# The up projections of a float32r transformer kernel: one moving operand of 512 columns for the activation's hi and lo halves

## The chip, the cores and the metric

The kernel runs on one core of one Trainium2 chip. The metric is the device time of one execution in microseconds; the kernel before takes 1380.37 us, the median of 3 runs (1379.97 to 1382.86).

## The reference

Three transformer layers over 256 tokens of width 1024 (batch 1), float32. The first block mixes a causal convolution, a stick-breaking attention and a cross-attention to a memory, then comes its feed-forward part; two hybrid layers (forgetting attention and retention) follow, each with the same feed-forward part between two layer norms. What the change touches is in all three:

```python
D_FF = 4 * D_MODEL                                                   # 4096
h2 = rms_norm(x, g_mlp[l])                                           # first block
x = x + jnp.square(jax.nn.relu(h2 @ w_up[l])) @ w_down[l]
...
hid = jnp.square(jax.nn.relu(jnp.einsum('bsd,df->bsf', x, w_ff1)))   # hybrid layers
ff = jnp.einsum('bsf,fd->bsd', hid, w_ff2)
return layernorm(DEEPNORM_ALPHA * x + ff, ln2_g, ln2_b)
```

## The kernel before

Every large product is computed in float32r with both operands split into a rounded high part and a remainder: w = w_hi + w_lo, x = x_hi + x_lo. Three products are kept, w_hi x_hi + w_lo x_hi + w_hi x_lo, so each 128 x 128 weight tile costs three matmuls of 256 moving columns (the 256 tokens).

Weights come in halves of 128 x 2048 (1 MB): eight contraction tiles of 256 columns for most products, four of 512 for the down projections. SP loads a half into one of two raw slots when the remainder of the half two before it is made (`lo_ready`). ACT copies it to `w_hi` (L251), DVE subtracts to `w_lo` (L619). `w_hi` and `w_lo` are rings of four halves; ACT overwrites a slot when TensorE has finished the half four before (`gemm_done`). All engines take the halves in one order written out by hand, and each engine takes its instructions in order.

PSUM is held as `gps` and `aps`, four banks of 512 columns each. `rows_first` (L1201) computes one up half, that is 256 rows of the hidden layer: `rows_part` (L1176) sends the output rows 0 to 127 to the left half of one `gps` bank and 128 to 255 to the right half, 48 matmuls on line L1182. With `split_count` (the first half after a norm) it goes through pairs of contraction tiles, both row blocks at a time: it waits for the pair's hi part, issues 8 matmuls, waits for its lo part, issues 4.

The feed-forward part (`ffn` on each engine) has 16 units, one per up half: on TensorE the halves 0 and 1 (units 0, 1), 2 and 3 (units 2, 3), then two down halves, and so on in turn: up pair, down pair, with the down pair always one up pair behind. Units 0 and 1 go into `gps` banks 0 and 1, units 2 and 3 into banks 2 and 3, and so on in turn; a bank is free when ACT has applied the relu of the unit four before (`ffn_relu`), so the first four wait for no bank. The down halves (L1274, L1277, L1279) accumulate in the four banks of `aps` over the whole feed-forward part and wait for `hidden`.

A unit's evacuation: ACT relu from PSUM to `staged` (L317), ACT square to `Q_hi` (L321); DVE squares `staged` into `hid_s` (L772) and subtracts `Q_hi` to give `Q_lo` (L776). On ACT and DVE the order is: split of halves 2 and 3; unit 0; split of half 4; unit 1; split of half 5; then in a loop unit, split, unit, split, split, split. In the hybrid layers DVE splits half 1 after the layer norm (L1152); in the first block all of that is done before the norm ends. `R_hi` and `R_lo`, the inputs of the up projections, come pair by pair from the norm: ACT writes hi (L286, L309), DVE lo (L681, L763).

Of the kernel before, what the change touches and what calls it, by code (L numbers as in the profile page):

```python
# [20 lines left out]
P = 128  # L21
# [53 lines left out]
def build(nc, mem_t, x_t, w1, w2, wf, par1, par2, con1, con2, out_t):  # L75
    with ExitStack() as ctx:
# [3 lines left out]
        def sem(name):  # L80
# [8 lines left out]
        R_hi, R_lo = sb("R_hi", [P, KT, T], F32R), sb("R_lo", [P, KT, T], F32R)  # L89
# [70 lines left out]
            mg mg_hi mg_lo ffn_relu ffn_sq ffn_hi hidden  # L160
# [82 lines left out]
        def _(act):  # L243
# [18 lines left out]
            def two(ap):  # L262
                return ap.rearrange("p (a t) -> p a t", a=2)
# [48 lines left out]
            def up(h, l, uu, par_, a, fresh=False):  # L312

                act.wait_ge(s["gemm_done"], h + (l + 1))
                if not fresh:
                    act.wait_ge(s["ffn_sq"], uu - 1)
                act.activation(staged[:, a, :], gps[:, 2 * par_ + a, :], ACT.Relu)\  # L317
                   .then_inc(s["ffn_relu"], 1)
                act.wait_ge(s["ffn_relu"], uu + 1)
                t0 = 4 * par_ + 2 * a  # L320
                act.activation(Q_hi[:, t0:t0 + 2, :], two(staged[:, a, :]), ACT.Square)\  # L321
                   .then_inc(s["ffn_hi"], 1)
# [290 lines left out]
        def _(dve):  # L613
# [155 lines left out]
            def up(uu, par_, a):  # L769
                t0 = 4 * par_ + 2 * a  # L770
                dve.wait_ge(s["ffn_relu"], uu + 1)
                dve.tensor_tensor(hid_s[:, a, :], staged[:, a, :], staged[:, a, :], ALU.mult)\  # L772
                   .then_inc(s["ffn_sq"], 1)
                dve.wait_ge(s["ffn_sq"], uu + 1)
                dve.wait_ge(s["ffn_hi"], uu + 1)
                dve.tensor_tensor(Q_lo[:, t0:t0 + 2, :], two(hid_s[:, a, :]),  # L776
# [398 lines left out]
        def _(pe):  # L1175
# [72 lines left out]
            def ffn(h0, l0, ub, split_count, ln=None):  # L1248

                def up(h, l, par_, free_sem, free_count):  # L1250
                    for a in range(2):

                        pe.wait_ge(free_sem, free_count + a)
                        rows_first(h, l + a, 2 * par_ + a, R_hi, R_lo,
                                   split_count if free_sem is not s["ffn_relu"] else None)
# [28 lines left out]
                relu = s["ffn_relu"]  # L1284
                for a in range(2):
                    rows_first(h0, l0 + a, a, R_hi, R_lo, split_count if a == 0 else None)
                for a in range(2):
                    rows_first(h0, l0 + 2 + a, 2 + a, R_hi, R_lo)
                down(h0, l0 + 4, 0, ub + 2, first=True)
                with pe.Fori(0, 3) as f:  # L1290
                    hf, uf = h0 + f * 8, ub + f * 4
                    up(hf, l0 + 6, 0, relu, uf + 1)
                    down(hf, l0 + 8, 1, uf + 4)
                    up(hf, l0 + 10, 1, relu, uf + 3)
# [151 lines left out]
            with pe.Fori(0, LAYERS) as ly:  # L1446
# [82 lines left out]
                pe.wait_ge(s["ffn_relu"], ly * 16 + 16)  # L1529
# [181 lines left out]
```

## Time and profile before

| | |
|---|---|
| median of 3 runs | 1380.37 us (1379.97 to 1382.86) |
| profiled execution: span (its own time is given as this alone) | 1381.2 us |
| TensorE busy (matmuls) | 1309.6 us, 95% |
| TensorE busy (weight loads) | 1257.4 us, 91% |
| DVE busy | 808.1 us, 59% |
| ACT busy | 647.6 us, 47% |
| mean granted TensorE clock | 0.984 |
| mean DMA rate | 155 GB/s |

A row of the groups reads: line, engine, operation, output and inputs, shapes, count, then busy time in us, mean ns of one, and the idle time of the engine just before. A matmul's duration holds its way through the array too, so that neighbours overlap; the pace of a stream is read from the distance of the starts. The feed-forward parts lie at about 451 to 640 us, 804 to 993 us and 1170 to 1359 us.

### The profile page before, as it was taken

To read this page: it belongs to the slowest core of one execution; us is meant where nothing else is said; L and a number is where in the kernel's file an instruction comes from. 1 tells how busy PE (TensorE), PEld (TensorE's weight loads), DVE (VectorE), ACT (ScalarE), POOL (GpSimd) and SP (SyncE) were. 2 spreads that over 40 slices of the span, in tenths; PEclk is the share of its full clock that TensorE was granted. 3 is DMA by queue.
4 is the path that set the end of the run, shared out by engine and by line. 5 is a ranking of instruction groups with operands and counts; after the bars stand their busy time and mean duration, and the time that the engine had idled before them with its cause. 6 is when DMAs were issued, how large, how long until landed. Compare 5 with 4: busy or idle time off the path is not lost.

```text
span 1381.2 us, 24664 instructions
## 1 busy us (share of the span) xinstructions
PE 1309.6 (95%) x10264; PEld 1257.4 (91%) x10264; DVE 808.1 (59%) x905; ACT 647.6 (47%) x722; POOL 0.2 (0%) x4
## 2 busy tenths in 40 slices
PE   5999999999999999999999979999889997999994
PEld 5999999999998999999888879999888896999994
DVE  5666965745555745454565666454656657655555
ACT  4565555664443534343434445444254444544443
POOL 0000000000000000000000000000000000000000
PEclk9999999999999999999999999999999999999998
DMA  6653444444554454553523226555233321565550
GB/s 222 214 184 123 157 149 150 157 149 156 183 184 153 153 188 178 186 209 125 183 92 123 92 100 224 195 178 187 91 143 136 116 99 61 183 214 186 179 183 31
DMA packets 34354, 214.58 MB, mean 155 GB/s; under 512 B 4576, under 2 KB 8672, under 8 KB 8800
## 3 DMA queue, kind: packets, MB, share of 16 engines
q1 hardware_dynamic: 34272, 213.37, 43.7%
q8 instruction: 65, 1.06, 0.3%
q14 instruction: 17, 0.14, 0.0%
HBM read 212.31 MB, written 1.05 MB: 154 GB/s over the span
## 4 chain that ended last, share of the span: by engine, by line
PE 85%; DVE 6%; ACT 3%; issue 3%; DMA 2%; SPq 0%; DVEq 0%; ACTq 0%
PE gps L1182 50%; PE aps L1279 7%; PE aps L1277 7%; PE aps L1274 7%; PE gps L1220 2%; PE gps L1221 2%; PE gps L1222 2%; DMA raw<-w 2%; DVE w_lo L619 1%; PE aps L1315 1%; ACT w_hi L251 1%; PE aps L1462 1%; PE aps L1483 1%; PE gps L1228 1%; ACT B L304 1%
## 5 line engine op out<-in xcount | busy, mean ns | idle before, releaser
L619 DVE TENSOR_TENSOR w_lo<-raw,w_hi 128x2048 fp32r<-128x2048 f32 x204 | 454.1, 2229 | 285.9 <-ACT w_hi L251 285.5
L251 ACT ACTIVATE w_hi<-raw 128x2048 fp32r<-128x2048 f32 x204 | 378.5, 1857 | 231.9 <-PE aps L1279 123.9
L1182 PE MATMUL gps<-R_hi,w_hi 128*128 128x256 f32 x896 | 238.2, 287 | 18.7 <-ACT R_hi L309 11.8
L1182 PE MATMUL gps<-H_hi,w_hi 128*128 128x256 f32 x896 | 241.3, 291 | 12.6 <-ACT H_hi L309 5.9
L1182 PE MATMUL gps<-R_hi,w_lo 128*128 128x256 f32 x896 | 236.9, 286 | 0.0
L1182 PE MATMUL gps<-H_hi,w_lo 128*128 128x256 f32 x896 | 236.5, 285 | 0.0
L1274 PE MATMUL aps<-Q_hi,w_hi 128*128 128x256 f32 x768 | 217.7, 283 | 0.0
L1277 PE MATMUL aps<-Q_lo,w_hi 128*128 128x256 f32 x768 | 217.3, 283 | 0.0
L1279 PE MATMUL aps<-Q_hi,w_lo 128*128 128x256 f32 x768 | 217.3, 283 | 0.0
L1182 PEld LDWEIGHTS gps<-R_hi,w_hi 128*128 128x128 f32 x896 | 175.0, 195 | 20.5 <-ACT R_hi L309 12.6
L1182 PEld LDWEIGHTS gps<-H_hi,w_hi 128*128 128x128 f32 x896 | 174.2, 194 | 15.1 <-issue 7.4
L1182 PE MATMUL gps<-H_lo,w_hi 128*128 128x256 f32 x896 | 179.9, 285 | 0.0
L1182 PE MATMUL gps<-R_lo,w_hi 128*128 128x256 f32 x896 | 179.5, 285 | 0.0
L1182 PEld LDWEIGHTS gps<-H_hi,w_lo 128*128 128x128 f32 x896 | 174.3, 195 | 1.1 <-issue 1.0
L1182 PEld LDWEIGHTS gps<-R_hi,w_lo 128*128 128x128 f32 x896 | 174.9, 195 | 0.0
L1274 PEld LDWEIGHTS aps<-Q_hi,w_hi 128*128 128x128 f32 x768 | 147.4, 192 | 0.1
L1277 PEld LDWEIGHTS aps<-Q_lo,w_hi 128*128 128x128 f32 x768 | 147.4, 192 | 0.1
L1279 PEld LDWEIGHTS aps<-Q_hi,w_lo 128*128 128x128 f32 x768 | 147.4, 192 | 0.0
L1182 PEld LDWEIGHTS gps<-H_lo,w_hi 128*128 128x128 f32 x896 | 140.3, 194 | 0.0
L1182 PEld LDWEIGHTS gps<-R_lo,w_hi 128*128 128x128 f32 x896 | 140.3, 194 | 0.0
L1182 PE MATMUL gps<-Q_hi,w_hi 128*128 128x256 f32 x320 | 85.1, 292 | 3.1 <-ACT Q_hi L601 3.1
L317 ACT ACTIVATE staged<-gps 128x512 f32<-128x512 f32 x48 | 28.5, 594 | 115.0 <-PE gps L1182 115.0
(229 smaller groups left out, 1654.2 us busy)
## 6 DMA issues: line engine op xcount, KB each, us to landing
raw<-w SPq DMA_DIRECT2D x198, 1024.0 KB, 4.8
B<-x_t SPq DMA_DIRECT2D x2, 512.0 KB, 4.5
B<-mem_t SPq DMA_DIRECT2D x1, 1024.0 KB, 7.7
B<-x_t SPq DMA_DIRECT2D x1, 1024.0 KB, 7.8
B<-con SPq DMA_DIRECT2D x1, 1024.0 KB, 6.8
out_t<-B SPq DMA_DIRECT2D x1, 1024.0 KB, 4.4
cst<-con SPq DMA_DIRECT2D x1, 320.0 KB, 4.8
raw<-wf SPq DMA_DIRECT2D x6, 16.0 KB, 1.6
```

Source lines behind the costliest of these rows:

```text
L251: act.activation(w_hi[:, ring(l), 0:n], raw[:, raw_slot(l), 0:n], ACT.Copy)\
L304: ins = act.activation(X[:, k, :], B1[:, k, :], ACT.Identity, bias=lpar[:, b + k:b + k + 1], scale=lpar[:, g + k:g + k + 1])
L317: act.activation(staged[:, a, :], gps[:, 2 * par_ + a, :], ACT.Relu)\
L619: dve.tensor_tensor(w_lo[:, ring(l), 0:n], raw[:, raw_slot(l), 0:n], w_hi[:, ring(l), 0:n].bitcast(F32), ALU.subtract)\
L1182: return pe.matmul(gps[:, bank_, nt * T:(nt + 1) * T], w[:, r, c:c + P], op[:, k, :], start=start, stop=stop, skip_group_check=True)
L1220: pe.matmul(out, xh, wh, start=(k == 0), stop=False)
L1221: pe.matmul(out, xh, wl, start=False, stop=False)
L1222: ins = pe.matmul(out, xl, wh, start=False, stop=(k == KT - 1))
L1228: ins = pe.matmul(out, ones, src[:, k, 0:T], start=(start and k == tiles[0]), stop=(stop and k == tiles[-1]))
L1274: pe.matmul(out, w_hi[:, r, c:c + P], hh, start=(first and k == 0 and nt % 2 == 0), stop=False, skip_group_check=True)
L1277: pe.matmul(out, w_hi[:, r, c:c + P], hl, start=False, stop=False, skip_group_check=True)
L1279: ins = pe.matmul(out, w_lo[:, r, c:c + P], hh, start=False, stop=(last and k == 3 and nt % 2 == 1), skip_group_check=True)
```

## The change

The two halves of the up projections' input become one tile `R` with hi and lo as its first index, so that `R[:, :, k, :]` is a moving operand of 512 columns: 256 of hi and 256 of lo. For each contraction tile and row block `up` issues a matmul of 512 columns with the `w_hi` tile, and one of 256 columns with the `w_lo` tile and `R_hi` into the left half of the same bank. A unit's two row blocks now fill two banks (unit a of a pair: banks 2a and 2a + 1), and the sum of the left and right halves is the projection. ACT copies the right halves of both banks to `staged`; DVE adds the left halves from PSUM into `hid_s`, then computes max(h, 0) h into `staged`; ACT copies that to `Q_hi`; DVE subtracts to `Q_lo`. TensorE waits, from the third unit of a feed-forward part on, for the DVE sum of the unit two before (`ffn_sum`). The first half of a feed-forward part waits, for each pair of contraction tiles, for hi and lo at once, in its first row block only, and goes through row block 0 entirely before row block 1.

```diff
--- before.py
+++ after.py
@@ -86,7 +86,8 @@
         w_lo = sb("w_lo", [P, 4, HALF], F32R)
 
         H_hi, H_lo = sb("H_hi", [P, KT, T], F32R), sb("H_lo", [P, KT, T], F32R)
-        R_hi, R_lo = sb("R_hi", [P, KT, T], F32R), sb("R_lo", [P, KT, T], F32R)
+        R = sb("R", [P, 2, KT, T], F32R)
+        R_hi, R_lo = R[:, 0, :, :], R[:, 1, :, :]
         Q_hi, Q_lo = sb("Q_hi", [P, KT, T], F32R), sb("Q_lo", [P, KT, T], F32R)
         B1, B2, B3 = (sb(f"B{i}", [P, KT, T]) for i in (1, 2, 3))
         B4 = sb("B4", [P, KT, T + 2])
@@ -157,7 +158,7 @@
             sb_z sb_sp sb_soft sb_lb sb_t sb_arg sb_e sb_a sb_o sb_ohi sb_olo
             hsq hn_sum hn_var hn_log hn_row hn_norm
             cx_s cx_max cx_exp cx_p cx_t cx_pt cx_o cx_oe ox_hi ox_lo
-            mg mg_hi mg_lo ffn_relu ffn_sq ffn_hi hidden
+            mg mg_hi mg_lo ffn_corr ffn_sum ffn_sq ffn_hi hidden
             f_cols f_gate f_logit f_sp f_m fx_s fx_l fx_max fx_e fx_p fx_t fx_pt fx_o fx_ohi fx_oe
             rt_mm rt_x rn_s rn_m rn_o rn_oe gn_mean gn_c gn_sq gn_var gn_v gn_log gn_y gn_hi gn_lo""".split()
         s = {n: sem(n) for n in names}
@@ -313,12 +314,12 @@
 
                 act.wait_ge(s["gemm_done"], h + (l + 1))
                 if not fresh:
-                    act.wait_ge(s["ffn_sq"], uu - 1)
-                act.activation(staged[:, a, :], gps[:, 2 * par_ + a, :], ACT.Relu)\
-                   .then_inc(s["ffn_relu"], 1)
-                act.wait_ge(s["ffn_relu"], uu + 1)
+                    act.wait_ge(s["hidden"], uu - 1)
+                act.activation(two(staged[:, a, :]), gps[:, 2 * a:2 * a + 2, T:2 * T], ACT.Copy)\
+                   .then_inc(s["ffn_corr"], 1)
+                act.wait_ge(s["ffn_sq"], uu + 1)
                 t0 = 4 * par_ + 2 * a
-                act.activation(Q_hi[:, t0:t0 + 2, :], two(staged[:, a, :]), ACT.Square)\
+                act.activation(Q_hi[:, t0:t0 + 2, :], two(staged[:, a, :]), ACT.Copy)\
                    .then_inc(s["ffn_hi"], 1)
 
             def ffn(h0, l0, ub, first=False):
@@ -768,12 +769,15 @@
 
             def up(uu, par_, a):
                 t0 = 4 * par_ + 2 * a
-                dve.wait_ge(s["ffn_relu"], uu + 1)
-                dve.tensor_tensor(hid_s[:, a, :], staged[:, a, :], staged[:, a, :], ALU.mult)\
-                   .then_inc(s["ffn_sq"], 1)
+                dve.wait_ge(s["ffn_corr"], uu + 1)
+                dve.tensor_tensor(two(hid_s[:, a, :]), gps[:, 2 * a:2 * a + 2, 0:T], two(staged[:, a, :]),
+                                  ALU.add).then_inc(s["ffn_sum"], 1)
+                dve.wait_ge(s["ffn_sum"], uu + 1)
+                dve.scalar_tensor_tensor(staged[:, a, :], hid_s[:, a, :], 0.0, hid_s[:, a, :],
+                                         ALU.max, ALU.mult).then_inc(s["ffn_sq"], 1)
                 dve.wait_ge(s["ffn_sq"], uu + 1)
                 dve.wait_ge(s["ffn_hi"], uu + 1)
-                dve.tensor_tensor(Q_lo[:, t0:t0 + 2, :], two(hid_s[:, a, :]),
+                dve.tensor_tensor(Q_lo[:, t0:t0 + 2, :], two(staged[:, a, :]),
                                   Q_hi[:, t0:t0 + 2, :].bitcast(F32), ALU.subtract)\
                    .then_inc(s["hidden"], 1)
 
@@ -1247,12 +1251,24 @@
 
             def ffn(h0, l0, ub, split_count, ln=None):
 
-                def up(h, l, par_, free_sem, free_count):
+                def up(h, l, summed, gate_at=None):
                     for a in range(2):
-
-                        pe.wait_ge(free_sem, free_count + a)
-                        rows_first(h, l + a, 2 * par_ + a, R_hi, R_lo,
-                                   split_count if free_sem is not s["ffn_relu"] else None)
+                        if summed is not None:
+                            pe.wait_ge(s["ffn_sum"], summed + a)
+                        pe.wait_ge(s["lo_ready"], h + (l + a + 1))
+                        r = ring(l + a)
+                        for nt in range(2):
+                            out = gps[:, 2 * a + nt, :]
+                            for k in range(KT):
+                                if gate_at is not None and a == nt == 0 and k % 2 == 0:
+                                    pe.wait_ge(gate_at[0], gate_at[2] + (k // 2 + 1))
+                                    pe.wait_ge(gate_at[1], gate_at[2] + (k // 2 + 1))
+                                c = k * 256 + nt * P
+                                pe.matmul(out, w_hi[:, r, c:c + P], R[:, :, k, :], start=(k == 0),
+                                          stop=False, skip_group_check=True)
+                                ins = pe.matmul(out[:, 0:T], w_lo[:, r, c:c + P], R_hi[:, k, :], start=False,
+                                                stop=(k == KT - 1), skip_group_check=True)
+                        ins.then_inc(s["gemm_done"], 1)
 
                 def down(h, l, par_, uu, first=False, last=False):
 
@@ -1281,17 +1297,14 @@
                                                 skip_group_check=True)
                         ins.then_inc(s["gemm_done"], 1)
 
-                relu = s["ffn_relu"]
-                for a in range(2):
-                    rows_first(h0, l0 + a, a, R_hi, R_lo, split_count if a == 0 else None)
-                for a in range(2):
-                    rows_first(h0, l0 + 2 + a, 2 + a, R_hi, R_lo)
+                up(h0, l0, None, split_count)
+                up(h0, l0 + 2, ub + 1)
                 down(h0, l0 + 4, 0, ub + 2, first=True)
                 with pe.Fori(0, 3) as f:
                     hf, uf = h0 + f * 8, ub + f * 4
-                    up(hf, l0 + 6, 0, relu, uf + 1)
+                    up(hf, l0 + 6, uf + 3)
                     down(hf, l0 + 8, 1, uf + 4)
-                    up(hf, l0 + 10, 1, relu, uf + 3)
+                    up(hf, l0 + 10, uf + 5)
                     down(hf, l0 + 12, 0, uf + 6)
                 down(h0, l0 + 30, 1, ub + 16, last=True)
 
@@ -1526,7 +1539,7 @@
                         ins.then_inc(s["gemm_done"], 1)
 
 
-                pe.wait_ge(s["ffn_relu"], ly * 16 + 16)
+                pe.wait_ge(s["ffn_sum"], ly * 16 + 16)
                 pe.wait_ge(s["resid"], ly * 8 + 8)
                 for l in range(LFFN):
                     if l >= LWO + 3:
```

## Rows read from the trace of the kernel before

**Rows 1.** The page: span, TensorE's share, and the chain that ended last.
```profile
span 1381.2 us, 24664 instructions
...
PE 1309.6 (95%) x10264; PEld 1257.4 (91%) x10264; DVE 808.1 (59%) x905; ACT 647.6 (47%) x722; POOL 0.2 (0%) x4
...
PE 85%; DVE 6%; ACT 3%; issue 3%; DMA 2%; SPq 0%; DVEq 0%; ACTq 0%
PE gps L1182 50%; PE aps L1279 7%; PE aps L1277 7%; PE aps L1274 7%; PE gps L1220 2%; PE gps L1221 2%; PE gps L1222 2%; DMA raw<-w 2%; DVE w_lo L619 1%; PE aps L1315 1%; ACT w_hi L251 1%; PE aps L1462 1%; PE aps L1483 1%; PE gps L1228 1%; ACT B L304 1%
```

**Rows 2.** Groups by line and shape: ACT's evacuation of the up halves.
```profile
L321 ACT ACTIVATE Q_hi<-staged 128x512 fp32r<-128x512 f32 x48 | 30.4, 633 | 1.5
L317 ACT ACTIVATE staged<-gps 128x512 f32<-128x512 f32 x48 | 28.5, 594 | 115.0 <-PE gps L1182 115.0
```

**Rows 3.** Timeline, TensorE within an up half: start us, us, engine line operation.
```profile
560.02 0.40 PE L1182 MATMUL gps<-R_lo,w_hi 128*128 128x256 f32 x2
560.26 0.28 PE L1182 MATMUL gps<-R_hi,w_hi 128*128 128x256 f32 x1
```

**Rows 4.** Timeline: eight plain fp32 matmuls of 256 columns (cross-attention scores).
```profile
263.14 1.89 PE L1351 MATMUL aps<-B 128*128 128x256 f32 x8
```

**Rows 5.** Timeline: float32r matmuls with weights of 8 columns (forget gates).
```profile
650.74 0.28 PE L1546 MATMUL gps<-H_hi,w_hi 128*8 128x256 f32 x1
...
652.96 0.28 PE L1547 MATMUL gps<-H_lo,w_hi 128*8 128x256 f32 x1
...
653.30 0.28 PE L1547 MATMUL gps<-H_lo,w_hi 128*8 128x256 f32 x1
```

**Rows 6.** Timeline, TensorE, layer 1: start of half 1, first down half.
```profile
813.26 0.38 PE L1182 MATMUL gps<-R_hi,w_hi 128*128 128x256 f32 x1 [1.15 <-DVE w_lo L619]
...
830.62 0.28 PE L1274 MATMUL aps<-Q_hi,w_hi 128*128 128x256 f32 x1
```

**Rows 7.** Timeline, DVE, layer 1: last `R_lo`, splits, unit 0.
```profile
810.31 0.69 DVE L763 TENSOR_TENSOR R_lo<-B,R_hi 128x512 fp32r<-128x512 f32 x1 [0.96 <-ACT R_hi L309]
810.92 4.49 DVE L619 TENSOR_TENSOR w_lo<-raw,w_hi 128x2048 fp32r<-128x2048 f32 x2
820.37 2.29 DVE L619 TENSOR_TENSOR w_lo<-raw,w_hi 128x2048 fp32r<-128x2048 f32 x1 [4.97 <-ACT w_hi L251]
822.58 0.68 DVE L772 TENSOR_TENSOR spb<-staged 128x512 f32<-128x512 f32 x1
```

**Rows 8.** Splits on ACT; DVE's three-operand form and PSUM read, 512 elements.
```profile
818.42 1.92 ACT L251 ACTIVATE w_hi<-raw 128x2048 fp32r<-128x2048 f32 x1 [6.33 <-DMA raw<-w]
...
821.59 1.92 ACT L251 ACTIVATE w_hi<-raw 128x2048 fp32r<-128x2048 f32 x1
...
777.67 0.68 DVE L636 SCALAR_TENSOR_TENSOR B<-B 128x512 f32<-128x512 f32 x1
...
L1048 DVE TENSOR_TENSOR B<-gps,B 128x512 f32<-128x512 f32 x8 | 5.5, 685 | 0.0
```

**Rows 9.** Timeline, layer 2: unit 0 on DVE, first down half.
```profile
1188.61 0.68 DVE L772 TENSOR_TENSOR spb<-staged 128x512 f32<-128x512 f32 x1
...
1196.83 0.28 PE L1274 MATMUL aps<-Q_hi,w_hi 128*128 128x256 f32 x1
```

**Rows 10.** Timeline, first block: last `R_lo`, split of half 4, first down half.
```profile
453.85 1.48 DVE L681 TENSOR_TENSOR R_lo<-B,R_hi 128x512 fp32r<-128x512 f32 x2
...
465.66 2.29 DVE L619 TENSOR_TENSOR w_lo<-raw,w_hi 128x2048 fp32r<-128x2048 f32 x1 [3.41 <-ACT w_hi L251]
...
476.74 0.28 PE L1274 MATMUL aps<-Q_hi,w_hi 128*128 128x256 f32 x1
```

**Rows 11.** Stretches (PE, PEld, DVE, ACT, POOL busy; PEclk; DMA; GB/s) and low clock.
```profile
801.57:804.98 3.41, 0.68 (x3) 0.69 (x4) 2.16 (x5) 2.46 (x5) 0.00 (x0) 0.50 0.00 0
665.03:668.45 3.42, 2.52 (x15) 1.75 (x14) 1.48 (x5) 3.02 (x5) 0.00 (x0) 1.00 0.64 206
...
806.17 1.05 PE L1182 MATMUL gps<-R_lo,w_hi 128*128 128x256 f32 x4
```

## The prediction

> **What bounds the kernel now.** I read the page first: shares of the engines and the chain of waits. TensorE is busy for 95% of the span and carries 85% of the chain that ended last; half of the chain is the line L1182, through which the up projections and most other projections run, and 21% are the three lines of the down projections [rows 1]. So the kernel goes as fast as TensorE takes its matmuls, and everything else counts only where TensorE waits for it. Then the groups by line: 48 evacuations of an up projection bank, 16 in each of three feed-forward blocks [rows 2]. I call one of these 48 units an up half. Then the timeline: inside an up half TensorE starts a 256-column matmul every 120 ns (two of them in 0.24 us, and the next starts 0.12 us after the second) [rows 3]; a half of 48 is 5.76 us. Last the timeline of ACT and DVE where a feed-forward block begins.
>
> **The price of the new pair.** For each contraction tile and each half of the rows, three matmuls with three weight loads (360 ns) become one of 512 columns and one of 256, with two loads. The columns streamed stay 768. What can be saved is whatever those 120 ns hold besides the streaming of 256 columns, and no row of before shows a 512-column matmul in this number format. Bounds:
> - Upper bound of the saving. A full fp32 matmul of 256 columns passes them twice, which is 512 columns: eight of them take 1.89 us, the last is 0.379 of it by the same view, so seven starts are 1.51 us apart and one takes 216 ns, though each has a weight load of 128 columns before it [rows 4]. So 512 columns can go by in 216 ns with the load of the next weights out of sight.
> - Which part of 120 ns is the load: with a weight load of 8 columns instead of 128 the same 256-column stream goes on average at (653.30 - 650.74) / 22 = 116 ns [rows 5]. So the load holds some 4 of the excess 13 ns over 256 / 2.4 GHz for certain, the rest may be either's.
> - So the second matmul of the new pair, 256 columns with the load for the next 512 behind it, keeps the form that costs 120 ns now. I take 216 + 120 = 336 ns, 24 ns less than now. That is nearest to the rows, because both halves of the sum are rows. If the queue hides the load of the small one too, it is 216 + 113 = 329 (113: the last three steps of the 8-column stretch, 652.96 to 653.30). If the 12 ns that 120 has over 216 / 2 belong in part to each column, the 512-column matmul takes 227 to 232 and the pair 347 to 352; if wholly, 240 + 120 = 360 and nothing is saved.
> - The Trainium skill (TensorE: Matmul & The Clock Gate, section "Wait — 56ns, not 53.3ns?") gives a fixed cost of about 2.5 ns a matmul above N / 2.4 GHz. By it alone the removed instruction would be worth 2.5 ns and not 24, and the old triple would have taken 328 ns; the trace has 360, so the rule does not describe this stream, but it does agree with the 216 ns of the double pass.
>
> Steady worth at 336: 16 pairs x 24 ns = 0.384 us a half, if TensorE never waits for anything new.
>
> **What is added on ACT and DVE.** Per up half ACT copies the correction halves (a 512-element evacuation, 0.59 us [rows 2]) and later copies to Q_hi (0.63, as the squares to Q_hi take now [rows 2]), as many instructions as now. DVE gets one more: an add that reads PSUM (0.69), then max-times (0.68), then the subtraction [rows 8]. ACT now has to wait between its two for both DVE instructions, about 1.5 us. In the middle of a block this costs nothing: TensorE works for 11.5 us on down halves between two pairs of up halves, and weight halves are split four ahead. I put these at zero there. DVE's three add up to 2.1 us and its weight split to 2.29 [rows 7], together less than the 5.4 us in which TensorE does the half.
>
> The new wait decides at the start of a block. Now the first four up halves go into four banks and wait for no evacuation. Afterwards one half takes two banks, so the third needs the first one's sum, the fourth the second one's.
>
> **Layer 1 of the second block.** On DVE the sum of unit 0 stands behind the splits of weight halves 1, 2 and 3 of the block. Splits 1 and 2 run from 810.92 for 4.49 us, so half 1 is ready at 813.2. Split 3 waits for a DMA and ACT (818.42) and runs from 820.37 to 822.66; the evacuation work of unit 0 begins at 822.58 [rows 7, 8]. TensorE then:
> - Half 0: all of rows 0 to 127 goes before rows 128 to 255, and each step waits for lo as well as hi. The last R_lo ends at 811.00 [rows 7]; tiles 6 and 7 take 2 x 0.336, then eight tiles of the second row block 2.69: ready at 814.5. Now half 1 starts at 813.26, after 1.15 us of idleness for its weights [rows 6], so half 0 could be that much longer for nothing; it costs 1.2 us.
> - Half 1: 5.38, to 819.9.
> - Half 2 needs the sum of unit 0: 822.58 + 0.69 and a signal, 823.4. TensorE stands 3.5 us. Then to 828.8.
> - Half 3 needs the sum of unit 1. DVE and ACT get there by a chain that TensorE does not shorten: sum 0.69, max-times 0.68, ACT Q_hi 0.63, ACT split of half 4 1.92 (its raw data is there by then: it is split at 821.59 now [rows 8]), DVE split 2.29, sum 0.69, 6.9 us from 822.6 with some 0.2 for signals: 829.7. Start 829.8, 1.0 us late; end 835.2.
> The first down half starts at 830.62 now [rows 6], so 4.6 us are lost by then. The other twelve up halves give back 12 x 0.384 = 4.6. Layer 1: 0.0.
>
> **Layer 2** the same from 1188.61 (DVE) and 1196.83 (PE) [rows 9]: half 3 starts at 1188.6 + 7.1 = 1195.75, ends at 1201.1, 4.3 us late; less 4.6: -0.3.
>
> **The first block** has its splits done earlier. Half 0 begins at low clock in both. The last two R_lo run from 453.85 for 1.48 us, so they end at 454.6 and 455.33 [rows 10]. In the new order two tiles of the first row block take 1.28 us at the low clock (768 columns at 1.2 GHz are 640 ns, times two): tiles 4 and 5 from 454.7 to 456.0, 6 and 7 to 457.1, with the clock rising late in them; plus 2.69 is 459.8. The sum of unit 1 follows the split that starts at 465.66: 468.6. TensorE asks for it at 459.8 + 10.75 = 470.5, no wait. Halves 1 to 3 end at 475.9, against 476.74 now [rows 10]: -0.8; twelve more: -4.6. Together -5.4.
>
> **Sum:** -5.4 + 0.0 - 0.3 = -5.7 us of a span of 1381.2, so 1375.5; the page gives the profiled execution by this span alone, and it lies 0.8 us above the median of the runs, 1380.37. On that median: 1374.7. I forecast 1375.
>
> The sum moves by 0.66 us for each ns of the pair (every half that isn't waited for has 16 pairs): 329 gives -10.6 (1370), 347 gives +1.4 (1382), 360 gives +10 (1390).
>
> **Rivals.**
> - *The columns set the pace, not the instructions.* 360 ns stay, and only the new waits at the block starts are left: 4.9 + 4.7 us in the two layers, 0.4 in the first block: 1390. For it: 120 ns hardly move when the load shrinks to 8 columns (116), so most of the excess is not the load [rows 5]. Against it: the double pass at 216 [rows 4], and 256 columns at the low clock take 213 ns (four in 1.05 us, of which the last is 0.41 by the rows of single ones there, so 0.64 for three) [rows 11], exactly 256 / 1.2 GHz, with no excess. It decides from a pair above 346 ns on: slower from about there.
> - *Half and half*, 345 to 352 ns: 1380 to 1385. Same or a little slower.
> - *The clock falls in the new stall.* In the first 6 us stall before a block the granted clock is 0.5 from 801.57 on [rows 11]; it also fell after 665.03:668.45 with TensorE busy for 2.52 of 3.42 us [rows 11]. The new stall of 3.5 us, for which no row has the answer, might do the same. Low clock from 823.4 for about 5.5 us of matmuls: 640 instead of 336 ns a pair, 2.6 us lost, of which the 1.0 us wait for the sum of unit 1 is swallowed: 1.7 a layer, 3.4 in all: 1378. Slower matmuls in half 0 by a later rise would be hidden by the wait for unit 0's sum in the layers.
> - *The load vanishes altogether*, 329 ns: 1370.
> - *The stalls stay away* because the queue order lets the sums through earlier: I see no way, as DVE takes its work in order. The clock apart, this and the waits in the middle of a block are the two places where my account of the queues can fail.
>
> **Chances.** 336 ns with the stalls: 0.40 (1373 to 1377). Clock: 0.15. 329: 0.12. Half and half: 0.17. Columns: 0.16. About 0.2% (2.8 us) is what a measurement of this kernel can tell from no change. Faster by more: 0.40 + 0.12 = 0.52. Same: most of the clock case and half of the middle case, 0.22. Slower: 0.26. Range: 1369 to 1388.
>
> **What would show it.** 512-column rows of the new matmul line at 216 ns to the next start and 256-column ones at 120 (or 240 and 120: the first rival). TensorE idle before an up half by a DVE sum, four times, 3.5 and 1.0 us in each layer, none in the first block. First down half at about 835 in layer 1, shifted by what the first block saved (5.4). Granted clock 1.0 through the stall. Idle for a sum anywhere else, or for weights in the middle of a block, would make the prediction wrong at the place where I put zero.

## The result, and the profile after

The changed kernel takes 1385.21 us, the median of 5 runs (1383.58 to 1386.63), against 1380.37, the median of 5 by now: slower by a ratio of 1.0033, 95% interval 1.0020 to 1.0045. The forecast was 1375.0, with 1369 to 1388 as its range and faster as the likelier side. The time lies in the range, on the other side of the kernel before.

The page after (span; busy; the chain by engine and by line), to be read beside [rows 1]:

```profile
span 1383.4 us, 23182 instructions
...
PE 1306.2 (94%) x9496; PEld 1213.9 (88%) x9496; DVE 839.1 (61%) x953; ACT 644.4 (47%) x722; POOL 0.2 (0%) x4
...
PE 83%; DVE 7%; ACT 4%; issue 3%; DMA 3%; SPq 0%; DVEq 0%; ACTq 0%
PE gps L1186 30%; PE gps L1267 12%; PE aps L1293 7%; PE aps L1295 7%; PE aps L1290 7%; PE gps L1269 6%; DMA raw<-w 3%; PE gps L1224 2%; PE gps L1225 2%; PE gps L1226 2%; ACT w_hi L252 1%; DVE w_lo L620 1%; PE aps L1328 1%; PE aps L1475 1%; PE aps L1496 1%
```

768 matmuls are gone (10264 to 9496), and TensorE's busy time fell by 3.4 us only, while DVE, ACT and DMA gained one point of the chain each. The groups by line and shape (busy time, mean ns of one, idle time before them and what ended it):

```profile
L1267 PE MATMUL gps<-R,w_hi 128*128 128x512 f32 x768 | 281.0, 408 | 24.2 <-DVE R L764 15.7 <-ACT R L287 5.3 <-DVE spb L773 3.2
L1269 PE MATMUL gps<-R,w_lo 128*128 128x256 f32 x768 | 218.8, 285 | 0.0
L776 DVE SCALAR_TENSOR_TENSOR staged<-spb 128x512 f32<-128x512 f32 x48 | 33.2, 692 | 1.7
L773 DVE TENSOR_TENSOR spb<-gps,staged 128x512 f32<-128x512 f32 x48 | 32.9, 685 | 7.9 <-ACT staged L318 7.9
L322 ACT ACTIVATE Q_hi<-staged 128x512 fp32r<-128x512 f32 x48 | 30.3, 632 | 123.4 <-DVE staged L776 123.4
```

The DVE and ACT durations are the ones forecast (0.69, 0.69, 0.63 us). The new wait for the DVE sum (`spb` is `hid_s`) costs TensorE 3.2 us of idleness in the whole span; ACT's long wait for L776 costs nothing. The mean of 408 ns is no pace. That is in the starts; timeline, TensorE in the middle of a block, to be read beside [rows 3]:

```profile
559.65 0.40 PE L1267 MATMUL gps<-R,w_hi 128*128 128x512 f32 x1
559.89 0.28 PE L1269 MATMUL gps<-R,w_lo 128*128 128x256 f32 x1
560.00 0.40 PE L1267 MATMUL gps<-R,w_hi 128*128 128x512 f32 x1
560.23 0.28 PE L1269 MATMUL gps<-R,w_lo 128*128 128x256 f32 x1
560.35 0.40 PE L1267 MATMUL gps<-R,w_hi 128*128 128x512 f32 x1
```

From 559.65 to 560.35 are two pairs, 350 ns each here; over whole halves the 512-column matmul is followed after 232, 236 or 241 ns, the small one after 113, 118 or 120, and the pair takes 353.3 ns. Before, three matmuls took 360; the forecast had 336. So a pair saves 6.7 ns, not 24.

Where the time went, by stages (us; each from the start of the last `R_lo` row on DVE to the first down half, then from there to the start of the last down half):

| | before | after | difference | forecast |
|---|---|---|---|---|
| first block, four halves | 22.89 | 22.20 | -0.7 | -0.8 |
| layer 1, four halves | 20.31 | 24.69 | +4.4 | +4.6 |
| layer 2, four halves | 20.33 | 24.81 | +4.5 | +4.3 |
| twelve further halves, three times | 138.24 each | 136.95 each | -3.9 | -13.8 |
| sum | | | +4.3 | -5.7 |

The medians differ by 4.8. The spans differ by only 2.2. In part that is 3.4 us of low clock that the profiled execution of before had outside these stages, some 1.7 us at half pace, and the one of after has not (granted clock 0.50 in before from 668.4 to 671.9, 1.00 in after from 455.5 to 796.8).

Layer 1 in detail, TensorE's starts of half 0 and every idle time up to the first down half, to be read beside [rows 6]:

```profile
801.44 0.76 PE L1267 MATMUL gps<-R,w_hi 128*128 128x512 f32 x1 [6.70 <-DVE R L764]
803.90 0.77 PE L1267 MATMUL gps<-R,w_hi 128*128 128x512 f32 x1 [0.84 <-DVE R L764]
805.81 0.76 PE L1267 MATMUL gps<-R,w_hi 128*128 128x512 f32 x1 [0.29 <-DVE R L764]
819.54 0.49 PE L1267 MATMUL gps<-R,w_hi 128*128 128x512 f32 x1 [1.31 <-DVE spb L773]
825.66 0.49 PE L1267 MATMUL gps<-R,w_hi 128*128 128x512 f32 x1 [0.22 <-DVE spb L773]
```

And DVE in the same stretch, to be read beside [rows 7]:

```profile
806.62 0.69 DVE L764 TENSOR_TENSOR R<-B,R 128x512 fp32r<-128x512 f32 x1 [0.95 <-ACT R L310]
807.22 4.49 DVE L620 TENSOR_TENSOR w_lo<-raw,w_hi 128x2048 fp32r<-128x2048 f32 x2
816.51 2.29 DVE L620 TENSOR_TENSOR w_lo<-raw,w_hi 128x2048 fp32r<-128x2048 f32 x1 [4.80 <-ACT w_hi L252]
818.72 0.68 DVE L773 TENSOR_TENSOR spb<-gps,staged 128x512 f32<-128x512 f32 x1
819.44 0.69 DVE L776 SCALAR_TENSOR_TENSOR staged<-spb 128x512 f32<-128x512 f32 x1
...
822.64 2.29 DVE L620 TENSOR_TENSOR w_lo<-raw,w_hi 128x2048 fp32r<-128x2048 f32 x1 [1.04 <-ACT w_hi L252]
824.85 0.69 DVE L773 TENSOR_TENSOR spb<-gps,staged 128x512 f32<-128x512 f32 x1
```

Half 0 ended at 812.4, and DVE stood idle for 4.80 us until 816.51. The sum of unit 0 could have run there; but it is queued behind the split of half 3, which waits for ACT and a DMA. It ends at 819.4 and TensorE's half 2 starts at 819.54. Half 3 starts at 825.66, after the sum of unit 1 (824.85 + 0.69).

Half 0 itself is slower than before: 10.98 us from its first start to half 1, against 8.96, of which 1.15 was the wait for weights. TensorE now waits 0.84 and 0.29 us in it, and the granted clock stays at 0.50 until 810.5, that is for 9.1 us after its first start; before, it was 4.1 us (804.30 to 808.4). The stall in front of half 2 hides this here. It comes back in the experiments.

### The profile page after: what moved, and what is told of

It reads as the page before. It is cut to its first block, busy times and chain, and to the rows that moved or that the text cites. A ratio compares the mean times of both kernels' runs of the same rounds, so it can differ in the third digit from the quotient of the medians.

```text
span 1383.4 us, 23182 instructions
## 1 busy us (share of the span) xinstructions
PE 1306.2 (94%) x9496; PEld 1213.9 (88%) x9496; DVE 839.1 (61%) x953; ACT 644.4 (47%) x722; POOL 0.2 (0%) x4
## 4 chain that ended last, share of the span: by engine, by line
PE 83%; DVE 7%; ACT 4%; issue 3%; DMA 3%; SPq 0%; DVEq 0%; ACTq 0%
PE gps L1186 30%; PE gps L1267 12%; PE aps L1293 7%; PE aps L1295 7%; PE aps L1290 7%; PE gps L1269 6%; DMA raw<-w 3%; PE gps L1224 2%; PE gps L1225 2%; PE gps L1226 2%; ACT w_hi L252 1%; DVE w_lo L620 1%; PE aps L1328 1%; PE aps L1475 1%; PE aps L1496 1%
## 5 line engine op out<-in xcount | busy, mean ns | idle before, releaser
L1267 PE MATMUL gps<-R,w_hi 128*128 128x512 f32 x768 | 281.0, 408 | 24.2 <-DVE R L764 15.7
L1269 PE MATMUL gps<-R,w_lo 128*128 128x256 f32 x768 | 218.8, 285 | 0.0
L1267 PEld LDWEIGHTS gps<-R,w_hi 128*128 128x128 f32 x768 | 147.8, 193 | 64.9 <-ACT R L310 14.1
L1269 PEld LDWEIGHTS gps<-R,w_lo 128*128 128x128 f32 x768 | 148.9, 194 | 0.0
L322 ACT ACTIVATE Q_hi<-staged 128x512 fp32r<-128x512 f32 x48 | 30.3, 632 | 123.4 <-DVE staged L776 123.4
L1186 PE MATMUL gps<-Q_hi,w_lo 128*128 128x256 f32 x320 | 82.2, 283 | 0.0
L268 ACT ACTIVATE B<-gps 128x512 f32<-128x512 f32 x52 | 30.8, 591 | 106.4 <-PE gps L1186 66.0
```

The source lines that it names most:

```text
L268: act.activation(dst, src, ACT.Copy, scale=scale).then_inc(s["evac"], 1)
L1186: return pe.matmul(gps[:, bank_, nt * T:(nt + 1) * T], w[:, r, c:c + P], op[:, k, :], start=start, stop=stop, skip_group_check=True)
L1267: pe.matmul(out, w_hi[:, r, c:c + P], R[:, :, k, :], start=(k == 0), stop=False, skip_group_check=True)
L1269: ins = pe.matmul(out[:, 0:T], w_lo[:, r, c:c + P], R_hi[:, k, :], start=False, stop=(k == KT - 1), skip_group_check=True)
```

## The experiments

The experiments were measured in three sets, each with runs of the kernel before beside it, and ratios are to the runs of the same set. The medians of the kernel before were 1380.96 (stream of matmuls by itself; only the waits; only the order; only the start of half 0), 1381.17 (first mixed stream; grouping by eight; both repairs; all together) and 1380.91 (second mixed stream; grouping by two). Every stage time below is from one profiled execution of each kernel. Code cuts are excerpts.

**The pace by itself.** A kernel that only streams matmuls, 64 of a kind.

> A kernel of its own, not a transformer: stretches of 64 matmuls with float32r operands, weights and moving operand already in SBUF, first with every other engine idle and at the end with ACT, DVE and the loads at work. Its output is not the reference's. It measures the disputed term, the start-to-start distance of a float32r matmul. Theory A (the moving columns of this format are slower than one per cycle at the 2.4 GHz level, whatever surrounds them): 512 columns 228 to 236 ns, 384 columns about 174, 256 columns with weights of 8 columns 113 to 117, and a contiguous 512-column operand as slow as the one in two pieces. Rival B (the two pieces of the operand, 8 KB apart, cost it): contiguous 512 columns 216 to 220 ns, two pieces 232 to 236. Rival C (traffic of ACT, DVE and DMA on SBUF): 216 to 220 ns in the quiet stretches, 232 to 236 in the last one with the traffic. Rival D (one PSUM bank written again and again): alternating banks takes 216, one bank 232. The pair of 512 and 256: 352 in A.

Measured: a stretch's pace is the distance from its first start to the next stretch's first start, over 64. Timeline, TensorE:

```profile
27.56 14.70 PE L88 MATMUL ps<-C,W 128*128 128x512 f32 x64
...
101.81 7.63 PE L100 MATMUL ps<-C,W 128*8 128x256 f32 x64
109.28 14.95 PE L102 MATMUL ps<-C,W 128*8 128x512 f32 x64
124.07 11.26 PE L104 MATMUL ps<-C,W 128*128 128x384 f32 x64
135.16 7.83 PE L106 MATMUL ps<-R,W 128*128 128x256 f32 x64
142.83 14.70 PE L108 MATMUL ps<-C,W 128*128 128x512 f32 x64
157.36 7.84 PE L110 MATMUL ps<-C,W 128*128 128x256 f32 x64
165.04 27.63 PE L112 MATMUL ps<-xs,ws 128*128 128x512 f32 x64
```

256 columns: (142.83 - 135.16) / 64 = 119.8 ns; 384: 173.3; 512: (157.36 - 142.83) / 64 = 227.0, whether the operand is in one piece or in two of 256, in one bank or in two, alone or with ACT, DVE and DMA at work. These lie on one line, 13.3 ns + columns / 2.4 GHz (120.0, 173.3, 226.7; away from the ends of a stretch that is the mean distance of the starts). So a float32r matmul has a fixed cost of some 13 ns, once per instruction; between 256 and 512 columns, columns as such cost nothing more. A shorter weight load does not remove it: with weights of 8 columns 256 take 116.7 ns and 512 take 231. Whether it would go without any load was not tried.

Plain fp32 with 512 columns (L112): the trace has 64 records for the kernel's 32 matmuls, so two for each, and a record starts every (27.63 - 0.59) / 63 = 429.2 ns. That is twice 512 columns at 2.4 GHz, 426.7, and 2.5 ns of fixed cost. The 216 ns of [rows 4] are 213.3 + 2.7 in the same way, and so were no price for a float32r matmul of 512 columns.

By the line, the new pair is 227 + 120 = 347 ns. But the two sizes in turn took 353.3 here too, in a kernel with nothing else in it. So 13 ns are saved and 6 or 7 given back.

**Only the waits.** The 512-column matmul is split in two of 256 again; banks, sums and waits stay.

```diff
-                                pe.matmul(out, w_hi[:, r, c:c + P], R[:, :, k, :], start=(k == 0), ...)
+                                pe.matmul(out[:, 0:T], w_hi[:, r, c:c + P], R_hi[:, k, :], start=(k == 0), ...)
+                                pe.matmul(out[:, T:2 * T], w_hi[:, r, c:c + P], R_lo[:, k, :], start=False, ...)
```

> The changed kernel with its 512-column matmul replaced by two of 256 columns, w_hi with R_hi into the left half and w_hi with R_lo into the right half of the same bank; the two banks a unit, the evacuation and all waits stay. Theory A: the merged matmul saves 6.7 ns a pair (353.3 against 360), so 48 x 16 x 6.7 = 5.1 us are lost, less 0.4 that the waits for sums in the two layers swallow: 1385.2 + 4.8 = 1390. A rival in which the pair costs nothing less than three and the whole +4.8 us of the change is the start of the blocks: 1385.

Measured: 1390.19 us, ratio 1.0066 (1.0052 to 1.0080); 120 ns from start to start again. So the wide operand is worth 5.0 us (1390.19 - 1385.21), and the rest of the change (banks, evacuation, waits, order of half 0) costs 9.2 (1390.19 - 1380.96). The slope of the prediction, 0.66 us for each ns of the pair, gives 4.4 for 6.7 ns.

**Only the order.** On ACT and DVE unit 0 goes between the splits of halves 2 and 3, and unit 1 ahead of that of half 4. The sum of unit 0 is then no longer behind the split of half 3, which waits for a DMA.

```diff
-                split(h0, l0 + 2)
-                split(h0, l0 + 3)
                 for a in range(2):
+                    split(h0, l0 + 2 + a)
                     up(...)
-                    split(h0, l0 + 4 + a)
+                split(h0, l0 + 4)
+                split(h0, l0 + 5)
```

> The changed kernel with ACT and DVE taking unit 0 before the split of weight half 3 and unit 1 before the split of half 4 at the start of each feed-forward part. Theory A (the sums stand behind the splits on DVE): the waits of 1.5 and 0.4 us before halves 2 and 3 go in both hybrid layers, the first block stays: 1385.2 - 3.8 = 1381.4. Rival (the waits only move: weights of half 3 or 4 are then late, as their DMA and split come later): 1385.

Measured: 1380.82 us, ratio 1.0001 (0.9992 to 1.0010); 4.4 less than the change. DVE in layer 1:

```profile
811.94 0.69 DVE L773 TENSOR_TENSOR spb<-gps,staged 128x512 f32<-128x512 f32 x1 [0.20 <-ACT staged L318]
...
816.61 2.29 DVE L620 TENSOR_TENSOR w_lo<-raw,w_hi 128x2048 fp32r<-128x2048 f32 x1 [1.80 <-ACT w_hi L252]
818.82 0.68 DVE L773 TENSOR_TENSOR spb<-gps,staged 128x512 f32<-128x512 f32 x1
```

The sum of unit 0 runs at 811.94 instead of 818.72, in what was idle time, that of unit 1 at 818.82 instead of 824.85, and the up halves 1, 2 and 3 follow each other with no gap (starts 811.02, 816.57, 822.12; first down half 827.66). So the sums' place in the queue is what cost the 4.4 us. It is not all that the block starts lost: layer 1 still takes 21.03 us from the start of the very last `R_lo` to the first down half and layer 2 22.75, against 20.32 and 20.33 before the change. In layer 2 no sum is waited for, but the low clock lasts for 9.0 us after half 0's first start (1167.09 to 1176.1), in layer 1 for 6.0.

**Only the start of half 0.** Half 0 goes through pairs of contraction tiles with both row blocks at a time, as before the change.

```diff
-                        for nt in range(2):
-                            for k in range(KT):
+                        tiles = ([(k + j, nt) for k in range(0, KT, 2) for nt in range(2) for j in range(2)]
+                                 if gated else [(k, nt) for nt in range(2) for k in range(KT)])
+                        for k, nt in tiles:
```

> The changed kernel with the first half of each feed-forward part going through both row blocks for each pair of contraction tiles, as before the change, but with the merged operand. Theory A: half 0 ends 1.5 to 3 us earlier in the layers, but half 2 still waits for unit 0's sum, which hangs on the DMA and split of half 3 and not on TensorE: the time is swallowed and 1385 stays (within 1 us). Rival (half 0's longer tail is what the change costs): 1380 to 1382.

Measured: 1388.40 us, ratio 1.0056 (1.0043 to 1.0070), 3.2 us more than the change: a miss. Layer 1, timeline, TensorE at the start of half 2:

```profile
820.01 0.79 PE L1269 MATMUL gps<-R,w_hi 128*128 128x512 f32 x1 [4.01 <-DVE spb L773]
```

The same on DVE:

```profile
819.20 0.68 DVE L773 TENSOR_TENSOR spb<-gps,staged 128x512 f32<-128x512 f32 x1
```

And the stretch after it (columns as in [rows 11]: busy times, granted clock, DMA):

```profile
820.10:825.00 4.90, 4.90 (x15) 4.21 (x16) 3.10 (x3) 2.91 (x3) 0.00 (x0) 0.50 0.61 217
```

Half 1 started at 810.08 and not at 812.42, and its last matmul 2.2 us earlier (815.71, 817.95); the sum came when it came, and the stall grew from 1.3 to 4.0 us. Late in it, at 818.7, the granted clock fell to 0.50 (1.2 GHz), and half 2 took 8.17 us (820.01 to 828.18) instead of 5.65. The same in layer 2 (stall of 4.05 us, low from 1190.7 to 1194.2). Against the changed kernel layer 1 lost 1.9 us, layer 2 1.0 and the first block 0.3. This is the third rival of the prediction: it did not happen in the changed kernel, whose stalls are 1.3 and 1.5 us (granted clock 1.00 from 819.60 to 825.10), and does happen when work in front of the stall gets faster.

**Where the last 6 ns go.** The next kernels look at the pair in itself, at grouping, and at the repairs together.

> A kernel of its own that only streams float32r matmuls with 128x128 weights and leaves the whole computation of the reference out. It asks where the 6.3 ns go by which a 512 and a 256 in turn (353.3 ns a pair in the last probe) exceed the two sizes by themselves (227.0 + 120.0 = 347). Theory 1, a change of the column count costs: streams of one size stay at 227.0 and 120.0 although they take their weights from two tensors in turn; two 512 and then two 256 take about 2 x 350; eight 512 and then eight 256 take 8 x 347.8; a 512 and a 256 in two banks, or with one weight tensor, still take 353; 384 and 256 in turn 173.4 + 120.0 + 6.3 = 299.7. Theory 2, the weights' tensor costs: the streams of one size rise to 230 and 123, and the pair with one weight tensor falls to 347. Theory 3, the same bank at two widths costs: the pair in two banks falls to 347. Besides, 320 columns should take 13.3 + 320 / 2.4 = 146.7 ns, and 128 columns 66.7 if nothing but the columns counts, 110 or more if the weight load of 128 columns does.

Measured (starts of the stretches, the first of 64 pairs each):

```profile
94.33 0.40 PE L105 MATMUL ps<-C,W 128*128 128x512 f32 x1
...
116.95 0.34 PE L108 MATMUL ps<-C,W 128*128 128x384 f32 x1
...
135.72 0.40 PE L111 MATMUL ps<-C,W 128*128 128x512 f32 x1
...
157.91 0.56 PE L114 MATMUL ps<-C,W 128*128 128x128 f32 x4
```

In two banks the pair still takes (116.95 - 94.33) / 64 = 353.4 ns. Streams of one size with weights from two tensors in turn stay at 227 and 120. 384 and 256 in turn take 293.3, the plain sum. With the same weight tile for both, the pair takes 346.7. Grouped by eight it is 349.2 (71.99 to 94.33), by two 348.3 (49.70 to 71.99); the expectations that have 349.2 for both are off by 0.9 there. (The next one has 354.2, 347.6 and 293.8 where these distances give 353.4, 346.7 and 293.3.) 320 columns take 146.7 as expected; 128 columns take 111 and not 66.7, so there something other than the columns is the limit. None of the three theories fits all of it.

> Streams of matmuls alone again, the reference's computation left out. In the last such kernel a 512 and a 256 in turn took 354.2 ns from two weight tensors, 347.6 with the same tile of one tensor for both; 384 and 256 in turn 293.8, the plain sum of the two sizes; grouping by two and by eight both 349.2. Neither of my theories covers that. Theory A, the same tile is what helps: a 512 and a 256 with different tiles of one tensor take 353, and so does the pair that reads its weights in the other tensors' roles. Theory B, one tensor helps: the pair with different tiles of one tensor takes 347. Theory C, only the pair of 512 and 256 is dear because the loads of weights fall badly against streams of these lengths: 512 + 384, 448 + 256 and 512 + 320 take the plain sums 400, 320 and 374 (by 13.3 ns + columns / 2.4 for each), or exceed them by 3 to 7. 512, 256, 256: 467 by the sum, 473 with one surcharge. The same tile twice in a stream of one size: 227.0 and 120.0, or less if a load is saved.

Measured, again by the starts of the stretches:

```profile
94.57 0.40 PE L100 MATMUL ps<-C,W 128*128 128x512 f32 x1
...
121.01 0.37 PE L103 MATMUL ps<-C,W 128*128 128x448 f32 x1
...
141.51 0.39 PE L106 MATMUL ps<-C,W 128*128 128x512 f32 x1
...
165.83 0.40 PE L109 MATMUL ps<-C,W 128*128 128x512 f32 x1
...
195.73 0.39 PE L113 MATMUL ps<-C,W 128*128 128x512 f32 x1
```

| in turn | per round, ns | sum of the sizes | excess |
|---|---|---|---|
| 512 + 384 | 413.1 | 400.3 | 12.8 |
| 448 + 256 | 320.3 | 320.0 | 0.3 |
| 512 + 320 | 380.0 | 373.6 | 6.4 |
| 512 + 256 + 256 | 467.2 | 467.0 | 0.2 |

A 512 and a 256 with different tiles of one tensor take 353.3, and so do they with the two tensors' parts exchanged; the same tile twice in a stream of one size saves nothing (227.0, 120.0). Within these streams B falls, A holds for the pair but not for streams of one size, and C holds in part: the excess comes when a 512 stands between single smaller ones, and is 0, 6 or 13 ns.

But the kernel shows that the same instructions can go either way. Timeline of the changed kernel, TensorE, first block, start of half 1:

```profile
459.13 0.40 PE L1267 MATMUL gps<-R,w_hi 128*128 128x512 f32 x1
459.36 0.28 PE L1269 MATMUL gps<-R,w_lo 128*128 128x256 f32 x1
459.48 0.39 PE L1267 MATMUL gps<-R,w_hi 128*128 128x512 f32 x1
459.71 0.27 PE L1269 MATMUL gps<-R,w_lo 128*128 128x256 f32 x1
459.82 0.40 PE L1267 MATMUL gps<-R,w_hi 128*128 128x512 f32 x1
```

Over this half a pair takes 346.7 ns, which is the plain sum (226.7 + 120.0), with 512 and 256 columns, two weight tensors and one bank as everywhere in this line. So it does in halves 1 to 3 of the first block (459.13, 464.68, 470.22, first down half 475.77: 5.55 us each) and in half 3 of layer 1; the other 41 halves behind a half 0 take 353.3. So sizes and operands do not fix the excess by themselves, and one stretch of a stream that comes out 6 ns cheaper, as the one with the same tile, does not show that the tile did it. The cause stays open.

**Grouping in the kernel.** Eight 512-column matmuls of a row block, then its eight of 256 columns:

```diff
                                 pe.matmul(out, w_hi[:, r, c:c + P], R[:, :, k, :], ...)
+                            for k in range(KT):
+                                c = k * 256 + nt * P
                                 ins = pe.matmul(out[:, 0:T], w_lo[:, r, c:c + P], R_hi[:, k, :], ...)
```

> Within a row block all eight 512-column matmuls go first and the eight of 256 columns after them. If the change of size is what costs 6.3 ns a pair, a pair falls from 353.3 to about 347.8, 5.5 ns x 16 pairs x 48 halves = 4.2 us less, of which the four halves at the start of the two layers return part to the wait for the first sum (about 0.3): 1385.2 - 3.9 = 1381.3. If the 6.3 ns come from anything else: 1385.2, no change. No size by which it gets slower in either account.

Measured: 1384.72 us, ratio 1.0026 (1.0017 to 1.0035), 3.4 over what was expected. The twelve further halves took 136.16 us against 136.95, 2.4 less in the three blocks; but the first block's four halves took 26.36 from their start against 24.16 (451.32 to 477.68; 451.61 to 475.77). In half 0 the small matmuls no longer fill the waits for the norm (two idle times of 0.20 us), and the low clock lasted to 458.7 there, against 455.5 in the changed kernel, which weighs more: 3.2 us at half pace are some 1.6 us. Whether the grouping made it last is not shown.

> The change with the matmuls of each two contraction tiles grouped, two of 512 and then two of 256, in every half. Grouping by eight was worth 0.8 us in the twelve further halves of each block and lost 2.2 us at the start of the first block, where in half 0 the 256-column matmuls no longer filled the waits for the norm. By twos they fill them again and the pair is as cheap (349.2 ns by the probe): 1384.7 - 2.2 = 1382.5 us, the two starts in the layers unchanged because the wait for the first sum takes up what is gained there. Rival, the start of the first block was chance: 1384.7.

Measured: 1382.74 us, ratio 1.0007 (0.9998 to 1.0015), as expected in the sum and not in its parts, so in part by luck: the first block got back 1.6 us and not 2.2 (24.76, 450.82 to 475.58; low clock to 455.8), the twelve further halves are a little faster still (136.0), and layer 2 lost 1.0. In layer 2 the clock fell again, after a stall of 1.91 us; timeline, TensorE:

```profile
1186.11 1.14 PE L1268 MATMUL gps<-R,w_hi 128*128 128x512 f32 x2 [1.91 <-DVE spb L773]
```

And the stretch after it:

```profile
1186.10:1191.00 4.90, 4.89 (x18) 4.17 (x19) 3.10 (x3) 2.91 (x3) 0.00 (x0) 0.65 0.65 217
```

**The repairs together**: the order, and half 0 with both row blocks; then the grouping too.

> Both repairs of the block start at once: sums of units 0 and 1 ahead of the weight splits on ACT and DVE (alone 1380.8, 4.4 less than the change), and half 0 in the order of the kernel before, both row blocks for each pair of contraction tiles (alone 1388.4, with half 1 starting 2.3 us earlier in each layer but the time lost in a stall of 4.3 us in which the clock fell). Theory, the second repair failed only by the stall behind it: with the sums early there is no stall, no fall of the clock, and the 2.3 us per layer and some 1 us in the first block stay: about 1376. Rival, half 1 then waits for its own weights, since the split of half 1 ends at 813.2 in any case: only the difference between 813.2 and 812.4 counts, nothing is gained or half 1 is the new wait: 1381. Second rival, the longer stretch of short bursts brings the low clock back later: over 1383.

Measured: 1376.48 us, ratio 0.9960 (0.9946 to 0.9974). The repair that cost 3.2 us by itself gains 4.3 on top of the other: half 1 starts at 810.32 in layer 1, the halves follow each other without a gap, and the first down half starts at 827.28. The stages are 20.21 us in layer 1 and 19.90 in layer 2, against 21.03 and 22.75 with the order alone. So most of this gain is in layer 2, and it goes with the clock: low for 6.1 us after half 0's first start there (1167.02 to 1173.1) instead of 9.0. In layer 1, where it was low for 6.0 us in both, the gain is 0.8.

> The two repairs and the grouping by size together (half 0 of each block grouped in twos by its gates). If they add up: 1376 - 4.2 = 1372, 0.6% below the kernel before. If the grouping is worth nothing: 1376. If the order of half 0 is worth nothing but the grouping is: 1377.

Measured: 1374.14 us, ratio 0.9940 (0.9927 to 0.9954), 2 over what was expected and faster than both kernels. Its page (span, chain):

```profile
span 1372.3 us, 23182 instructions
...
PE 85%; DVE 6%; ACT 4%; issue 3%; DMA 2%; SPq 0%; DVEq 0%; ACTq 0%
```

Timeline, TensorE, its first down half in layer 1:

```profile
825.14 0.28 PE L1295 MATMUL aps<-Q_hi,w_hi 128*128 128x256 f32 x1
```

By stages, here from the start of the very last `R_lo`: the first block's four halves -0.8 against the kernel before, layer 1 (19.82 against 20.32) and layer 2 -0.5 each, the twelve further halves 136.16 against 138.24, three times, -6.2: -8.0, and the medians differ by 7.0. The grouping is worth 2.3 of them.

## Why the prediction was wrong

- **The step that failed is the price of the new pair**: "I take 216 + 120 = 336 ns". It measured 353.3, and the twelve further halves, where no wait changed, gave 3.9 us in the three blocks and not 13.8. 216 was read from plain fp32 ([rows 4]), whose fixed cost is 2 to 3 ns; float32r has 13, and the 512-column matmul costs 227. (The reading of [rows 4] was loose besides: they are four matmuls of the kernel with two records each, and 216 ns is a record.) The bound was a row, but of another number format, and it was taken for the value because it was exact. The prediction's middle case named 227 to 232 and 347 to 352, for a reason (cost in part of each column) that is false: the excess is per instruction. The second error is that a pair was priced as the sum of two streams of one size. In turn they cost 353.3 in most halves (6.3 more), which no row of before could show, and why is open. By the prediction's own slope the term was off by 17.3 x 0.66 = 11.4 us, and -5.7 + 11.4 = +5.7, near the +4.8 measured. (That slope gives -10.3 and +1.6 for its rivals of 329 and 347 ns, where it has -10.6 and +1.4; nothing hangs on it.)
- **What the removed instruction is worth.** The Trainium skill (TensorE: Matmul & The Clock Gate, section "Wait — 56ns, not 53.3ns?") has a fixed cost of about 2.5 ns. Plain fp32 agrees (429.2 - 426.7 = 2.5), float32r does not (13.3 at 256, 320, 384 and 512 columns). The prediction had found this difference in the old triple and then gave the new matmul the fp32 price all the same.
- **The first rival** (360 ns, 1390) was wrong in its mechanism, since columns are not what costs; its number is the one that the kernel with the split operand gives, 1390.19.
- **The waits at the block starts were right** in place and in sum: +4.4 and +4.5 against 4.6 and 4.3, four waits for a DVE sum, none in the first block, none in the middle. The first one was 1.5 us (from 818.07, the end of half 1, to 819.54) and not 3.5, because halves 0 and 1 ended later: from the end of the last `R_lo` to the end of half 1 10.8 us, against 8.9 forecast. The prediction priced the rest of half 0 in the layers at the full clock, but the clock was low until 810.5, 3.2 us after that `R_lo` (some 1.6 us); the dearer pair makes the rest. The sum comes at a time set by DVE and ACT, so what TensorE loses before it is swallowed. So the size of the wait was wrong and the time of the first down half right.
- **The clock** stayed at 1.00 in the stalls of the changed kernel, as the main case had it. The runs with stalls of 1.9 and 4.0 us show that the rival was a real one; the stall of 3.5 us that the main case forecast lies between them and did not come, so that the clock held is in part luck.
- **The costs put at nothing** (the third DVE instruction, ACT's long wait) were nothing: no idle time for a sum outside the block starts.
- **First block**: -0.7 against -0.8, by two errors that cancel: halves 1 to 3 gave 0.6 us (5.55 against 5.76 each) and not 1.2, and half 1 started 4.1 us after the end of the last `R_lo` (455.04 to 459.13), not 4.5. Its twelve further halves gave 1.3, not 4.6.

## What to carry to other kernels

Price an instruction by rows of its own number format, and of its own neighbours: a stream of one size says nothing for certain of two sizes in turn. When an evacuation is made longer or waited for sooner, look where it is queued: here it stood behind a split that waited for a DMA while its engine was idle for 4.8 us, and moving it forward gave back 4.4 of the 8.9 us that the two layers' starts had lost. The rest lay in half 0, in its order and in the low clock that lasted longer with it, out of sight until then. A faster stage in front of a fixed stall gives nothing and can bring the clock down; the same repair was worth +3.2 us with the stall and -4.3 without it.

## What the runs showed of the hardware

- Float32r matmuls of one size in a stream: 13.3 ns + columns / 2.4 GHz from 256 to 512 columns; 128 columns take 111 ns. Plain fp32: 2.5 ns of fixed cost a record, with two records a matmul and each as long as twice its columns (429.2 ns for 512, 216 for 256). At the low clock a pair of 512 and 256 columns takes 640 ns (820.81 to 821.45 in the kernel with the changed half 0), exactly 768 / 1.2 GHz: no fixed cost and no excess there.
- Weights of 8 columns instead of 128 make 256 moving columns faster (116.7 against 120.0 ns) and 512 slower (231 against 227).
- In the streams 512 columns in turn with one smaller matmul cost 6.3 ns more than the sum with 256 or 320 and 12.8 with 384; 384 with 256, 448 with 256, and 512 with two of 256 cost nothing more. In the changed kernel 512 and 256 in turn took 346.7 ns in four halves and 353.3 in the others that ran at full clock. Grouping leaves 1.6 ns a pair over the plain sum by two (348.3) and 2.5 by eight (349.2).
- The granted clock fell to 0.50 around stalls of 1.9 us (once) and 4.0 us (twice) with TensorE busy at full clock before. It did not around stalls of 1.1 to 1.5 us, nor around one of 1.77 us (before 821.48 in the kernel with only the waits).
- At the start of a layer's feed-forward part the clock stayed low for 3.0 to 6.1 us after half 0's first start in the four kernels that take both row blocks at a time (before: 4.1 and 3.1), and for 6.0 to 11.2 us in the five that take row block 0 first (changed kernel: 9.1 and 8.7). Each of these is one profiled execution.
